# Layer two's adaLN chunks in two parts, six weight places before the first gather, and other latent norm chains

## The chip, the core and the metric

The kernel runs on one core of one Trainium2 chip. The metric is the time of one execution on the device in microseconds (us). Five engines work beside each other: TensorE (PE; its weight loads are listed as PEld), VectorE (DVE), ScalarE (ACT), GpSimd (POOL) and SyncE (SP), which here only issues transfers. The 16 DMA engines move the data.

## The reference

Two networks of two layers each, one behind the other, on 256 tokens of 1,024 float32 numbers. The first has a hybrid mixer and a PEER layer, in which each token picks 128 of 16,384 rows of two tables:

```python
def first_block(x, c, ...):
    c_act = jax.nn.silu(c)
    for l in range(DEPTH):                      # 2
        mod = c_act @ ada_w[l] + ada_b[l]       # 1024 x 6144
        sh1, sc1, g1, sh2, sc2, g2 = jnp.split(mod, 6, axis=-1)
        h = _modulate(x, sh1, sc1)
        mix = _hybrid_mixer(h, ...)
        x = _layer_norm(DEEPNORM_ALPHA * x + (1.0 + g1) * mix, ln1_g[l], ln1_b[l])
        h = _modulate(x, sh2, sc2)
        ffn = _peer(h, peer_wq[l], peer_k1[l], peer_k2[l], peer_u[l], peer_v[l])
        x = _layer_norm(DEEPNORM_ALPHA * x + (1.0 + g2) * ffn, ln2_g[l], ln2_b[l])
```

The second works on its result (the latents) and on 256 context tokens, which leave it after its first layer:

```python
h = modulate(rmsnorm(x, norm_pre_mix[i]), sh1, sc1)
mix = concat([windowed_gqa_with_context(...), fourier_mix(...)]) @ w_out[i]
x_mid = x + g1 * rmsnorm(mix, norm_post_mix[i])
hf = modulate(rmsnorm(x_mid, norm_pre_ffn[i]), sh2, sc2)
x = x_mid + g2 * rmsnorm(swiglu(hf, w_gate[i], w_up[i], w_down[i]), norm_post_ffn[i])
# and the same for xc, with csh1, csc1, cg1, ..., in layer 0
```

## The kernel before

Each engine has its own program, written out in one order; semaphores tie them together. In the code `b0` and `b1` are the layers of the first network, `c0` and `c1` the context's passes through the second, `l0` and `l1` the latents'.

**Order.** The head is `block1(0)`: mixer and routing of b0 for both tiles of 128 tokens. Then come the gathers: for each of four (layer, tile) pairs, 128 rows per token of table u (`dots`, L1611 on) and 128 of table v (`sums`, L1625 on). GpSimd issues one gather of 128 rows, 0.5 MB, for each pick (L1019) into one of nine slots; six of them are the tile `RING`. DVE uses the slots in order and gives each back. Beside this, DVE takes one step of another block's generator after fixed rounds of four picks (`stage`, the dictionaries at the end of the vector program): first c0's mixer while (0, tile 0) sums, then b1 tile by tile (`tile1`), then the rest of c0. When the gathers are over, l0 and l1 run alone.

**Weights.** PE asks for each weight chunk with `weight()` (L350); a chunk is up to 2,048 numbers on 128 partitions, 1 MB. The chunks lie in `W`, which has `NW = 3` places: chunk n goes to place n % 3, and SP issues it when chunk n - 3 has been read. SP's queue is the list `stream` in the order in which PE's program met `weight()`, `load_rows()` and `load()`; an entry that waits holds up all behind it. `load_rows` (L374) brings two rows of 1,024 to all partitions of `ROWS`; they wait until the two before have been read (`rows_read`).

**adaLN.** `ada(p, aw, whos, groups, beside)` (L419) multiplies the condition with 512 columns of the modulation weights at a time: a group is two chunks. FIRST and SECOND are four groups each (shift and scale of the first and second half of the layer), GATE1 and GATE2 two each. ACT copies each group's row to `ROWT`, PE turns it into columns (L437) or spreads it over the partitions (L443), and ACT copies that. With `beside`, a group also waits for a pick (`pace`, L414).

**Places that the change touches.** The keys of the routing (`SKN`) are loaded by an entry of `stream` behind b0's SECOND, with a wait for `(filled, len(order))`, that is for all banks opened so far (L577 to L579). b1's FIRST and SECOND run together, 16 chunks, before c0's mixer (L944); ACT takes seven of their copies, then `gelu(0, 0)`, then the rest (L1391 on). The latent norms are `stats`, `normalise` and `residual` (L1437, L1460, L2177): `bn_stats` of the rows, `bn_aggr`, the square of the mean, a root on ACT, a reciprocal, products with the gate row, an addition over both tiles, and then the same for the next norm. Between l0's two halves PE also has GATE1 of l1, and before l1 GATE2.

## Time and profile before

| | us |
|---|---|
| median of three runs (2920.5 to 2934.6) | 2928.4 |
| the profiled execution | 2932.3 |
| its span in the trace | 2930.5 |
| head, to the first gather | 267 |
| gathers and what runs beside them, to layer one's latents | 267 to 2,160 |
| latent blocks | 2,160 to 2,930 |

Busy over the span: PE 65%, DVE 62%, POOL 36%, ACT 13%. No engine is busy throughout, so the stretches have to be read one by one. In a timeline a row is one instruction or several alike in sequence; the number in brackets is the idle time of the engine before the first of them and what ended it. A DMA share of 1.03 or 1.04 is what the trace shows when all 16 engines are at work. The granted clock has two levels, 1.2 and 2.4 GHz, shown as 0.5 and 1.0.

### The profile page before, as it was taken

The page shows a single profiled execution, that of the slowest core. Times are in us where ns is not written, and L with a number is a line of the kernel's source. Part 1 is how long each engine was busy: PE and PEld are TensorE (multiplying, and loading weights), DVE is VectorE, ACT ScalarE, POOL GpSimd, SP SyncE. Part 2 cuts the span into 40 slices and gives each one's busy share as a digit, 9 for nine tenths or more (in the row PEclk, how much of TensorE's full clock was granted, in tenths as well). Part 3 has the DMA queues.
Part 4 walks back from the last instruction along what each step waited for, and adds up shares of the span by engine and source line. Part 5 has one row for each costly group of instructions (what it writes and reads, how often), then busy time and mean ns, then how long its engine had stood idle before and what let it go on. Part 6 is the DMA issues. An engine that isn't in the chain of part 4 may idle for free.

```text
span 2930.5 us, 23625 instructions
## 1 busy us (share of the span) xinstructions
PE 1910.9 (65%) x8197; PEld 1343.1 (46%) x8197; DVE 1819.2 (62%) x3305; ACT 367.6 (13%) x818; POOL 1064.6 (36%) x1045
## 2 busy tenths in 40 slices
PE   7889444356553363544444457868178999997998
PEld 4668111144442151132242145743157786476873
DVE  1434999678778878988879986676854200243001
ACT  1311101013102011012111010000013100030000
POOL 1002444457555555755566755455610000000000
PEclk9989655567766675867778877989579999998999
DMA  7367999989999999999999999999861544512443
GB/s 245 99 207 236 399 399 400 400 315 386 335 344 405 400 401 401 362 335 397 401 401 397 341 330 392 374 403 406 328 235 37 189 149 153 187 60 86 156 146 115
DMA packets 361766, 860.86 MB, mean 294 GB/s; under 512 B 23720, under 2 KB 148912, under 8 KB 361520
## 3 DMA queue, kind: packets, MB, share of 16 engines
q0 software_dynamic: 148000, 537.07, 47.8%
q1 hardware_dynamic: 213648, 322.29, 31.6%
q8 instruction: 65, 1.06, 0.1%
q14 instruction: 53, 0.43, 0.0%
HBM read 858.23 MB, written 1.05 MB: 293 GB/s over the span
## 4 chain that ended last, share of the span: by engine, by line
PE 36%; DMA 34%; DVE 15%; issue 10%; POOL 3%; ACT 2%; SPq 0%; DVEq 0%; ACTq 0%
PE bank L912 13%; DMA RING<-in_peer_v,EX 8%; PE bank L397 7%; DMA W<-in_ada_w 5%; DMA W<-in_w_ada 5%; PE bank L926 5%; DMA RING<-in_peer_u,EX 5%; DMA WORK<-in_peer_v,EX 3%; PE bank L406 3%; DMA W<-in_w_up 2%; POOL RING L1019 2%; DVE ACC L1639 2%; PE bank L429 2%; DMA W<-in_w_gate 2%; DVE hrows L1639 1%
## 5 line engine op out<-in xcount | busy, mean ns | idle before, releaser
L1019 POOL DMA_INDIRECT RING<-in_peer_u,EX x343 | 326.4, 952 | 569.6 <-DVE EX L1596 255.6
L912 PE MATMUL bank<-HT,W 128*128 128x256 f32 x2112 | 490.8, 397 | 54.1 <-DMA W<-in_w_up 28.9
L912 PEld LDWEIGHTS bank<-HT,W 128*128 128x128 f32 x2112 | 421.6, 200 | 123.1 <-DMA W<-in_w_up 32.2
L1019 POOL DMA_INDIRECT RING<-in_peer_v,EX x341 | 379.2, 1112 | 239.0 <-DVE hrows L1639 119.5
L1621 DVE SCALAR_TENSOR_TENSOR ACC<-RING,hrows 128x1024 bf16<-128x1024 f32 x343 | 406.2, 1218 | 79.4 <-DMA RING<-in_peer_u,EX 77.9
L429 PE MATMUL bank<-W,CACT 128*32 128x512 f32 x768 | 166.3, 969 | 271.0 <-DMA W<-in_w_ada 130.7
L397 PE MATMUL bank<-W,HT 128*128 128x256 f32 (+1 forms) x1120 | 250.1, 386 | 20.5 <-ACT HT L1071 7.4
L385 PE MATMUL bank<-consts,XN 128*128 128x128 f32 x208 | 44.6, 398 | 309.8 <-DVE XN L1710 149.5
L397 PEld LDWEIGHTS bank<-W,HT 128*128 128x128 f32 x1120 | 215.9, 195 | 53.9 <-issue 11.3
L926 PE MATMUL bank<-W,WORK 128*128 128x512 f32 x528 | 229.3, 597 | 14.3 <-DVE WORK L2209 14.3
L2209 DVE TENSOR_TENSOR WORK<-WORK,bank 128x256 f32<-128x256 f32 x66 | 27.2, 420 | 321.6 <-ACT WORK L1366 321.6
L1019 POOL DMA_INDIRECT WORK<-in_peer_v,EX x171 | 188.3, 1101 | 102.9 <-DVE hrows L1639 40.1
L1621 DVE SCALAR_TENSOR_TENSOR ACC<-WORK,hrows 128x1024 bf16<-128x1024 f32 x169 | 201.2, 1218 | 38.3 <-DMA WORK<-in_peer_u,EX 37.8
L1639 DVE SCALAR_TENSOR_TENSOR hrows<-RING,ACTS,hrows 128x1024 f32<-128x1024 f32 x154 | 198.2, 1287 | 37.1 <-DMA RING<-in_peer_v,EX 35.9
L1639 DVE SCALAR_TENSOR_TENSOR ACC<-RING,ACTS,ACC 128x1024 f32<-128x1024 f32 x155 | 198.6, 1281 | 32.6 <-DMA RING<-in_peer_v,EX 32.2
L1019 POOL DMA_INDIRECT WORK<-in_peer_u,EX x169 | 161.2, 954 | 156.9 <-DVE ACC L1621 132.3
L429 PEld LDWEIGHTS bank<-W,CACT 128*32 128x32 f32 x768 | 20.9, 135 | 364.3 <-DMA W<-in_w_ada 117.7
L385 PEld LDWEIGHTS bank<-consts,XN 128*128 128x128 f32 x208 | 38.8, 212 | 316.2 <-DVE XN L1710 151.7
L926 PEld LDWEIGHTS bank<-W,WORK 128*128 128x128 f32 x528 | 100.9, 192 | 141.3 <-issue 125.9
L621 PE MATMUL bank<-HT,W 128*128 128x128 f32 x832 | 118.4, 311 | 52.0 <-DMA W<-in_peer_wq 29.9
L621 PEld LDWEIGHTS bank<-HT,W 128*128 128x128 f32 x832 | 115.9, 226 | 56.1 <-DMA W<-in_peer_wq 26.6
L1054 ACT ACTIVATE WORK<-bank 128x512 f32<-128x512 f32 (+5 forms) x161 | 85.7, 546 | 434.2 <-PE bank L397 135.7
(343 smaller groups left out, 2289.2 us busy)
## 6 DMA issues: line engine op xcount, KB each, us to landing
W<-in_ada_w SPq DMA_DIRECT2D x48, 1024.0 KB, 13.5
W<-in_w_ada SPq DMA_DIRECT2D x48, 1024.0 KB, 16.5
W<-in_w_in SPq DMA_DIRECT2D x35, 1024.0 KB, 10.8
W<-in_w_gate SPq DMA_DIRECT2D x33, 1024.0 KB, 5.4
W<-in_w_up SPq DMA_DIRECT2D x33, 1024.0 KB, 5.6
W<-in_w_down SPq DMA_DIRECT2D x33, 1024.0 KB, 5.0
W<-in_peer_wq SPq DMA_DIRECT2D x24, 1024.0 KB, 16.5
W<-in_w_o SPq DMA_DIRECT2D x12, 1024.0 KB, 11.8
```

The source lines that it names most:

```text
L385: mm = pe.transpose(b[0:rows, j * P:(j + 1) * P], a, ident)
L397: mm = pe.matmul(b[:, t * 256:t * 256 + cols], hT[:, k, t * P:(t + 1) * P], w[:, k, 0:cols], start=(k == 0), stop=(k == K - 1))
L406: mm = pe.matmul(b[:, j * S:(j + 1) * S], w[:, k, j * P:(j + 1) * P], hT[:, k, :], start=(k == 0), stop=(k == DC - 1))
L429: mm = pe.matmul(b[32 * k:32 * k + 32, :], CACT[:, 4 * c + k, :], w[:, k, :], start=(c == 0), stop=(c == 1), skip_group_check=True)
L621: mm = pe.matmul(b[:, at:at + P], w[:, k, at:at + P], HT[:, 4 * c + k, T], start=first, stop=(c == 1 and k == 3), skip_group_check=True)
L912: mm = pe.matmul(bs[j][:, g * S:(g + 1) * S], w[:, k, j * P:(j + 1) * P], HT[:, k, :], start=(k == 0 and g == 0), stop=(k == DC - 1 and g ...
L926: mm = pe.matmul(bs[2 * t + hf][:, :], GU[:, 2 * c + k, t * P:(t + 1) * P], w[:, k, hf * 512:(hf + 1) * 512], start=(c == 0 and k == 0), s ...
L1019: gp.indirect_dma_start(SLOT[g % NS], None, rows, bass.IndirectOffsetOnAxis(EX[:, t, k:k + 1], 0))\
L1054: free(name, A(out_, b[:, :] if src is None else src(b), ACT.Copy, scale=scale))
L1621: ve.scalar_tensor_tensor(out=JUNK[:, g % 2, :], in0=SLOT[g % NS], scalar=1.0, in1=HB[:, :], op0=ALU.mult, op1=ALU.mult, accum_out=ACTS[:, ...
L1639: ins = ve.scalar_tensor_tensor(out=acc, in0=SLOT[g % NS], scalar=ACTS[:, k:k + 1], in1=acc, op0=ALU.mult, op1=ALU.add)
L2209: free(("gu", p, f), ve.tensor_tensor(GU[:, f, :], SG[:, f % 2, :], b[:, S:2 * S], ALU.mult))
```

## The change

1. **Six places.** For the first 36 chunks there are six places: the three of `W` and three more, each of two slots of `RING`. Chunk n waits for chunk n - 6. From chunk 36 on it is three again. The first six gathers wait for chunks 33 to 35. X, the late constants and ctx keep their places in SP's queue but for X (behind chunk 6, not 3) and the constants (behind 12, not 9).
2. **Keys.** b0's keys are issued by GpSimd when the last bank of b0's mixer is filled.
3. **b1's adaLN.** FIRST runs where FIRST and SECOND ran, with other paces; SECOND runs behind c0's mixer and ahead of tile one. `ln2` rows, asked for after it, move behind it in SP's queue.
4. **Latent norms.** The gate row is multiplied while the banks are read, one product per tile adds to X (`gated_residual`), and the next norm's squares are summed on ACT, tile by tile (`root_of_squares`). The output's store waits for both tiles.

```diff
@@ -102,6 +103,7 @@
+        WIDE = 36
@@ -252,7 +254,7 @@
-        w_landed = [sem(f"w_landed{i}") for i in range(NW)]
+        w_landed = [sem(f"w_landed{i}") for i in range(2 * NW)]
@@ -286,6 +288,20 @@
+        def place(n):
...
+            return n % (2 * NW) if n < WIDE else n % NW
...
+        def landed(n):
...
+            if n < WIDE:
+                return w_landed[place(n)], 16 * (n // (2 * NW) + 1)
+            return w_landed[place(n)], 16 * (WIDE // (2 * NW) + (n - WIDE) // NW + 1)
...
+        def held_before(n):
...
+            return n - 2 * NW if n < WIDE + NW else n - NW
@@ -351,11 +367,13 @@
-                view = W[:, n % NW, 0:k * cols].rearrange("p (k c) -> p k c", k=k)
+                at = place(n)
+                room = W[:, at, :] if at < NW else RING[:, 2 * (at - NW):2 * (at - NW) + 2, :].rearrange("p s n -> p (s n)")
+                view = room[:, 0:k * cols].rearrange("p (k c) -> p k c", k=k)
...
-                pe.wait_ge(w_landed[n % NW], 16 * (n // NW + 1))
+                pe.wait_ge(*landed(n))
@@ -574,9 +592,6 @@
-                load([(SKN[:, :, 0, :], d["peer_k1"][l].rearrange("h n d -> n h d")),
-                      (SKN[:, :, 1, :], d["peer_k2"][l].rearrange("h n d -> n h d"))],
-                     mark("skn", p), (filled, len(order)))
@@ -941,10 +956,11 @@
-            ada("b1", d["ada_w"][1], [0], FIRST + SECOND, beside=lambda i: gather(0, 0, 0, 5 * i + 80))
+            ada("b1", d["ada_w"][1], [0], FIRST, beside=lambda i: gather(0, 0, 0, 10 * i + 64))
...
+            ada("b1", d["ada_w"][1], [0], SECOND)
@@ -970,23 +986,23 @@
-                if e is chunks[NW]:
+                if e is chunks[2 * NW]:
...
-                if e is chunks[9]:
+                if e is chunks[12]:
...
-                    if n >= NW:
-                        sp.wait_ge(*chunks[n - NW]["free"])
-                    sp.dma_start(e["dst"], e["src"]).then_inc(w_landed[n % NW], 16)
+                    if held_before(n) >= 0:
+                        sp.wait_ge(*chunks[held_before(n)]["free"])
+                    sp.dma_start(e["dst"], e["src"]).then_inc(landed(n)[0], 16)
...
-            sp.wait_ge(mark("xu", "l1"), 2)
+            sp.wait_ge(mark("xu", "l1"), 2 * NT)
@@ -1006,6 +1022,10 @@
+            gp.wait_ge(filled, banks["mx", "b0", 3][0] + 1)
+            for e, keys in enumerate((d["peer_k1"], d["peer_k2"])):
+                gp.dma_start(SKN[:, :, e, :], keys[0].rearrange("h n d -> n h d")).then_inc(mark("skn", "b0"), 16)
@@ -1016,6 +1036,8 @@
+                            if g < NR:
+                                gp.wait_ge(*[e for e in stream if "dst" in e][WIDE - NW + g // 2]["free"])
@@ -1056,6 +1078,14 @@
+            def root_of_squares(p, i):
...
+                for t in range(NT):
+                    act.wait_ge(mark("xu", p), NT * (i - 1) + t + 1)
+                    do(A(XN[:, t, :], X[:, t, :], ACT.Square, accum_out=VE[:, t, 1:2]))
+                settle()
+                do(A(SD[:, :, 0], VE[:, :, 1], ACT.Sqrt, bias=const("eps"), scale=1.0 / D), mark("std", p if i == 1 else "l1"))
@@ -1282,7 +1312,10 @@
-                root(p, 1)
+                if p == "l1":
+                    root_of_squares("l0", 2)
+                else:
+                    root(p, 1)
@@ -1350,12 +1383,14 @@
-                root(p, 2)
+                root(p, 2 if p != "l1" else 1)
...
-                root(p, 3)
+                    root(p, 3)
+                else:
+                    root_of_squares(p, 1)
@@ -1388,12 +1423,10 @@
-            second = ada("b1", [0], FIRST + SECOND)
-            for _ in range(7):
-                next(second)
+            all_of(ada("b1", [0], FIRST))
...
-            all_of(second)
...
+            all_of(ada("b1", [0], SECOND))
@@ -1434,6 +1467,17 @@
+            def mean_squares(p, parts):
...
+                settle()
+                for t in range(NT):
+                    do(ve.bn_aggr(MV[:, t, :], parts[:, t, :, :]))
+                settle()
+                do(ve.tensor_tensor(VE[:, :, 0], MV[:, :, 0], MV[:, :, 0], ALU.mult))
+                settle()
+                do(ve.scalar_tensor_tensor(out=VE[:, :, 0], in0=VE[:, :, 0], scalar=RMS_EPS, in1=MV[:, :, 1],
+                                           op0=ALU.add, op1=ALU.add), mark("var", p))
@@ -2046,6 +2087,20 @@
+            def inverse_root(p, i):
...
+                ve.wait_ge(mark("std", p), i)
+                do(ve.reciprocal(RSD[:, :, 0], SD[:, :, 0]))
+                settle()
...
+            def rows_over_root(p, i):
...
+                inverse_root(p, i)
+                for t in range(NT):
+                    ins = ve.tensor_scalar(XN[:, t, :], X[:, t, :], RSD[:, t, 0:1], None, ALU.mult)
+                    do(ins, mark("y", p)) if t else do(ins)
+                settle()
@@ -2062,7 +2117,10 @@
-                normalise(p, 1, xs, RMS_EPS, True, XN, mark("y", p))
+                if p == "l1":
+                    rows_over_root("l1", 1)
+                else:
+                    normalise(p, 1, xs, RMS_EPS, True, XN, mark("y", p))
@@ -2172,30 +2230,42 @@
-                        free(("mx", p, j), ve.tensor_copy(XN[:, :, j * 256:(j + 1) * 256], two(b[:, :])))
+                        free(("mx", p, j), ve.tensor_tensor(XN[:, :, j * 256:(j + 1) * 256], two(b[:, :]),
+                                                            over_tiles(GA[:, gs[0], j * 256:(j + 1) * 256], 256), ALU.mult))
...
-                def residual(i, g, parts=None, names=None):
...
-                    if not names:
-                        settle()
-                    stats(p, i, XN, RMS_EPS, True, parts)
+                def residual(i, g):
...
+                    settle()
+                    stats(p, i, XN, RMS_EPS, True)
...
-                        for hf in range(2) if names else (0,):
-                            c = slice(hf * 512, (hf + 1) * 512) if names else slice(0, D)
-                            src = BK[banks[names[2 * t + hf]][0] % RB][:, :] if names else XN[:, t, :]
-                            ins = ve.scalar_tensor_tensor(out=XN[:, t, c], in0=src, scalar=RSD[:, t, 0:1], in1=GA[:, g, c],
-                                                          op0=ALU.mult, op1=ALU.mult)
-                            free(names[2 * t + hf], ins) if names else do(ins)
+                        do(ve.scalar_tensor_tensor(out=XN[:, t, :], in0=XN[:, t, :], scalar=RSD[:, t, 0:1], in1=GA[:, g, :],
+                                                   op0=ALU.mult, op1=ALU.mult))
...
-                residual(2, gs[0], ST4 if who == "l" else None)
...
+                def gated_residual(i, parts, names=()):
...
+                    mean_squares(p, parts)
+                    for k, name in enumerate(names):
+                        c = slice((k % 2) * 512, (k % 2 + 1) * 512)
+                        free(name, ve.tensor_tensor(XN[:, k // 2, c], wait_full(ve, name)[:, :], GA[:, gs[1], c], ALU.mult))
+                    settle()
+                    inverse_root(p, i)
+                    for t in range(NT):
+                        do(ve.scalar_tensor_tensor(out=X[:, t, :], in0=XN[:, t, :], scalar=RSD[:, t, 0:1], in1=X[:, t, :],
+                                                   op0=ALU.mult, op1=ALU.add), mark("xu", p))
...
+                    residual(2, gs[0])
...
-                normalise(p, 3, xs, RMS_EPS, True, XN, mark("y", p))
+                    normalise(p, 3, xs, RMS_EPS, True, XN, mark("y", p))
+                else:
+                    gated_residual(2, ST4)
+                    rows_over_root(p, 3)
```

SP's queue around b0's SECOND chunks and keys, before:

```order
L978 DMA XC<-in_ctx 128x2x1024
L983 DMA W<-in_w_o 128x8x256 x2
L988 DMA ROWS<-in_ln_g 128x1024
L988 DMA ROWS<-in_ln_b 128x1024
L983 DMA W<-in_ada_w 128x4x512 x8
L988 DMA WORK<-in_peer_k 128x8x128 x2
L983 DMA W<-in_peer_wq 128x8x256 x8
L983 DMA W<-in_ada_w 128x4x512 x4
```

and after:

```order
L999 DMA RING<-in_w_o 128x8x256 x2
L994 DMA XC<-in_ctx 128x2x1024
L999 DMA W<-in_w_o 128x8x256 x2
L1004 DMA ROWS<-in_ln_g 128x1024
L1004 DMA ROWS<-in_ln_b 128x1024
L999 DMA W<-in_ada_w 128x4x512
L999 DMA RING<-in_ada_w 128x4x512 x3
L999 DMA W<-in_ada_w 128x4x512 x3
L999 DMA RING<-in_ada_w 128x4x512
L999 DMA RING<-in_peer_wq 128x8x256 x2
L999 DMA W<-in_peer_wq 128x8x256 x6
```

The keys are gone from it, and between mixer and routing the chunks alternate between both kinds of places.

ACT from the copies of c0's mixer to the root of layer one's norm (128x1); ROWT and CR are adaLN copies, the roots are `SD<-VE`. Before:

```order
L1054 ACTIVATE XN<-bank 128x2x256 x4
L1058 ACT_TABLE_LOAD
L1058 ACTIVATE SD<-VE 128x2
L1063 ACTIVATE SD<-VE 128x1
L1269 ACT_TABLE_LOAD
```

After:

```order
L1076 ACTIVATE XN<-bank 128x2x256 x4
L1080 ACT_TABLE_LOAD
L1080 ACTIVATE SD<-VE 128x2
L1076 ACTIVATE ROWT<-bank 128x512 x2
L1076 ACTIVATE CR<-bank 128x4
L1076 ACTIVATE ROWT<-bank 128x512
L1076 ACTIVATE CR<-bank 128x4
L1076 ACTIVATE ROWT<-bank 128x512
L1076 ACTIVATE CR<-bank 128x4 x2
L1093 ACTIVATE SD<-VE 128x1
```

The eight adaLN copies of b1's SECOND now stand between c0's root (128x2) and layer one's root (128x1), which DVE's tile one begins with.

DVE in the middle of l1, from the last copy of the mixer's bank to the rows of the next norm. Before:

```order
L2175 COPY XN<-bank 128x2x256
L1447 BN_AGGR MV<-ST 128x2 x2
L1450 TENSOR_TENSOR VE<-MV 128x2
L1452 SCALAR_TENSOR_TENSOR VE<-VE,MV 128x2
L1457 RECIPROCAL RSD<-SD 128x2
L2188 SCALAR_TENSOR_TENSOR XN<-XN,RSD,GA 128x1024 x2
L2192 TENSOR_TENSOR X<-X,XN 128x2048
L1444 BN_STATS ST<-X 128x6 x4
L1447 BN_AGGR MV<-ST 128x2 x2
L1450 TENSOR_TENSOR VE<-MV 128x2
L1452 SCALAR_TENSOR_TENSOR VE<-VE,MV 128x2
L1457 RECIPROCAL RSD<-SD 128x2
L1464 TENSOR_SCALAR XN<-X,RSD 128x1024 x2
```

After:

```order
L2233 TENSOR_TENSOR XN<-bank,GA 128x2x256
L1474 BN_AGGR MV<-ST 128x2 x2
L1476 TENSOR_TENSOR VE<-MV 128x2
L1478 SCALAR_TENSOR_TENSOR VE<-VE,MV 128x2
L2093 RECIPROCAL RSD<-SD 128x2
L2258 SCALAR_TENSOR_TENSOR X<-XN,RSD,X 128x1024 x2
L2093 RECIPROCAL RSD<-SD 128x2
L2100 TENSOR_SCALAR XN<-X,RSD 128x1024 x2
```

The addition over both tiles and the second statistics are gone; ACT has two Squares in their place.

## Rows read from the trace of the kernel before

**Rows 1.** The page's slices: 40 equal parts of 73.3 us, busy tenths, DMA rate.

```profile
DVE  1434999678778878988879986676854200243001
...
DMA  7367999989999999999999999999861544512443
GB/s 245 99 207 236 399 399 400 400 315 386 335 344 405 400 401 401 362 335 397 401 401 397 341 330 392 374 403 406 328 235 37 189 149 153 187 60 86 156 146 115
```

**Rows 2.** Timeline of PE, head: start us, us, instruction, count, [idle before <-releaser].

```profile
32.04 1.52 PE L429 MATMUL bank<-W,CACT 128*32 128x512 f32 x8 [1.19 <-DMA W<-in_ada_w]
...
148.44 1.87 PE L429 MATMUL bank<-W,CACT 128*32 128x512 f32 x8 [3.69 <-DMA W<-in_ada_w]
...
152.91 2.78 PE L385 MATMUL bank<-consts,WORK 128*128 128x128 f32 x24
...
197.59 1.92 PE L429 MATMUL bank<-W,CACT 128*32 128x512 f32 x16
...
221.55 3.65 PE L385 MATMUL bank<-consts,XN 128*128 128x128 f32 x16
228.05 3.68 PE L385 MATMUL bank<-consts,WORK 128*128 128x128 f32 x16 [2.85 <-DMA WORK<-in_peer_k]
```

**Rows 3.** Timelines of ACT and of DVE, head.

```profile
147.04 0.57 ACT L1054 ACTIVATE ROWT<-bank 128x512 f32<-128x512 f32 x1
...
212.70 1.53 DVE L1466 TENSOR_SCALAR XN<-X,MV,RSD 128x1024 f32<-128x1024 f32 x2
```

**Rows 4.** Timeline of PE, layer two's adaLN chunks beside the gathers.

```profile
484.42 1.93 PE L429 MATMUL bank<-W,CACT 128*32 128x512 f32 x8 [5.64 <-DMA W<-in_ada_w]
...
536.70 1.93 PE L429 MATMUL bank<-W,CACT 128*32 128x512 f32 x8 [5.30 <-DMA W<-in_ada_w]
...
596.80 1.93 PE L429 MATMUL bank<-W,CACT 128*32 128x512 f32 x8 [5.53 <-DMA W<-in_ada_w]
```

**Rows 5.** Timeline of DVE, norm rows, residual, layer one's root.

```profile
580.95 1.28 DVE L1639 SCALAR_TENSOR_TENSOR ACC<-WORK,ACTS,ACC 128x1024 f32<-128x1024 f32 x1 [0.76 <-DMA WORK<-in_peer_v,EX]
600.80 4.63 DVE L2034 TENSOR_TENSOR GA<-GA,ROWS 128x1024 f32<-128x1024 f32 x4 [18.57 <-DMA ROWS<-in_norm_post_ffn]
...
785.86 2.47 DVE L1444 BATCH_NORM_STATS2 ST<-XN 128x6 f32<-128x512 f32 x4 [11.63 <-ACT XN L1054]
...
810.50 0.16 DVE L1693 RECIPROCAL RSD<-SD 128x1 f32<-128x1 f32 x1
```

**Rows 6.** Windows: us, busy of PE, PEld, DVE, ACT, POOL, clock, DMA share, GB/s.

```profile
786.00:805.00 19.00, 0.00 (x0) 0.00 (x0) 18.31 (x24) 1.34 (x3) 4.54 (x4) 0.61 0.70 252
805.00:844.00 39.00, 14.18 (x57) 9.69 (x58) 38.37 (x73) 6.49 (x13) 24.07 (x25) 0.63 0.79 286
```

**Rows 7.** Timelines of PE and of SP's queue before layer two's first tile.

```profile
821.89 1.97 PE L385 MATMUL bank<-consts,XN 128*128 128x128 f32 x8 [36.89 <-DVE XN L1710]
...
768.30 17.10 SPq L983 DMA_DIRECT2D W<-in_w_in  x3
```

**Rows 8.** Timeline of PE, starts behind three latent norms.

```profile
2297.87 2.90 PE L443 MATMUL bank<-ROWT,consts 128*128 128x512 f32 x4
...
2547.01 1.97 PE L385 MATMUL bank<-consts,XN 128*128 128x128 f32 x16
...
2683.53 3.67 PE L385 MATMUL bank<-consts,XN 128*128 128x128 f32 x16 [12.70 <-DVE XN L1464]
```

**Rows 9.** Timeline of DVE, layer two's middle and last latent norm.

```profile
2676.09 2.29 DVE L2192 TENSOR_TENSOR X<-X,XN 128x2048 f32<-128x2048 f32 x1
2678.42 2.47 DVE L1444 BATCH_NORM_STATS2 ST<-X 128x6 f32<-128x512 f32 x4
...
2921.05 2.73 DVE L2188 SCALAR_TENSOR_TENSOR XN<-bank,RSD,GA 128x512 f32<-128x512 f32 x4
2923.81 2.29 DVE L2192 TENSOR_TENSOR X<-X,XN 128x2048 f32<-128x2048 f32 x1
```

**Rows 10.** Timeline of ACT, an elementwise step over 1,536 columns.

```profile
112.01 1.48 ACT L1123 ACTIVATE WORK<-WORK 128x1536 f32<-128x1536 f32 x1
```

## What the change does to the time

> **What bounds the kernel now.** I read the page's slices first. They show three stretches [rows 1]: a head up to about 300 us, in which the DMA engines are mostly part idle; the gathers of the two PEER layers, up to about 2,130 us, in which the DMA row stands at 8 or 9 almost throughout and carries about 400 GB/s; and the latent blocks of the second network, to 2,930 us, where PE stands at 9 or 7. So each part of the change has to be costed in its own stretch. In the head the timeline of PE shows which waits end last. In the gathers a wait of DVE alone costs nothing if DMA works on through it, since the bytes are the same: there I ask how much DMA idle time goes away. In the latent blocks the gaps of PE between two blocks of matmuls count, and in each of them what ends last.
>
> **1. Six weight places and the keys, in the head.** Start: PE's last wait for a chunk of the first adaLN group ends at 32.04 us and is 1.19 us long [rows 2]. Until then DMA has had to bring the same eight chunks and X in either order, so more places bring nothing: 0, at most the 1.2 us of that wait, and as much in loss if X behind three more chunks mattered.
>
> GATE1: PE waits 3.69 us for a chunk until 148.44, works at the lower of its clocks, and begins the probabilities' transposes at 152.91 [rows 2]. The chunk had to wait for a place. With six it is there. What is late next is ACT, which is in exponentials and copies the first of the two rows at 147.04, done at 147.6 [rows 3]. The gate rows' broadcasts need that copy and took 2.8 us, so the transposes begin at about 150.3: 152.9 - 150.3 = 2.6 us; bounds 1.5 and 3.7 (the wait itself).
>
> SECOND: the transposes of the second modulated input start at 221.55, right behind the last SECOND group [rows 2]; their input XN was ready at 212.70 + 1.53 = 214.2 [rows 3]. With six places five of the eight chunks are there when PE arrives at 197.59 [rows 2], and the other three follow it at one transfer each, so the group ends near 212 and XN becomes the later one. That is 221.55 - 214.2 = 7.3 us. The ln1 rows stand ahead of the SECOND chunks in SP's queue and wait for the old rows to be read, which is over well before the mixer's last product, so the chunks are not blocked for long.
>
> Keys: PE then waits 2.85 us more for the keys until 228.05 [rows 2]. Before, their load stood in SP's queue behind a wait for the whole SECOND group; now GpSimd issues them when the mixer's last bank is filled (197.6), 16 us before XN. Its queue holds nothing else ahead of the first gather. That is 2.8 us; if the moved load were no earlier, 0. The places themselves cost nothing: they lie in the ring of gathers, whose first six uses now wait for chunks that are read before the first scores, so before any routing.
>
> Head: 2.6 + 7.3 + 2.8 = 12.7 us (10 to 17; the upper end if PE, less interrupted, also keeps its higher clock). From the first routing on DVE is busy and DMA full, both shifted alike, so the gain stays.
>
> The Trainium skill (page "DMA: Bandwidth & Descriptors", section "Issuing engines are not separate DMA queues") says that starting DMAs on several engines only saves the sequencer's time for issuing. By that the move of the keys to another queue would be worth nothing and the sum 2.8 us less. The rows speak for the other reading: it is the wait ahead of the load, not the engines that move it, that goes.
>
> **2. Four chunk pairs behind the context's mixer.** Now: the b1 chunks start in DMA-bound time. FIRST's first chunk is used at 484.42, its last at 536.70, SECOND's last at 596.80: 7.5 us each beside gathers [rows 4]. The norm rows stand behind all 16 in SP's queue, so DVE waits 18.57 us for them, until 600.80; just before, its sums come every 2.04 us (0.76 of it waiting) [rows 5]. After: the rows come behind FIRST, by about 545. The wait goes, and the last five sums before it come at 1.3 us, the 0.5 MB of a gather at 400 GB/s, instead of 2.04: 18.6 + 3 = 21.6. In the wait all nine slots had filled, a start that is now missing; I take off 1.6. The mixer's steps are tied to rounds of DVE's sums, so all of it, to the residual at 785.86, comes 20 us earlier (17 to 23).
>
> What is paid back: the eight chunks, 8.4 MB or 21 us at 400 GB/s, now have to pass between the mixer and layer two's first tile. In that place DMA has room: its share is 0.70 for 19 us and 0.79 for 39 us where a full one reads 1.03, so 19 x (1 - 0.70/1.03) + 39 x (1 - 0.79/1.03) = 6.1 + 9.1 = 15.2 us of idle [rows 6], and PE stands 36.9 us before tile one's transposes at 821.89 [rows 7]. I let the chunks use 12 of the 15; 21 - 12 = 9 us remain (6 to 21). On ACT the new copies stand ahead of the root that DVE uses at 810.50 [rows 5]. Chunks take the places from 768.30 on as the mixer's are read, three by 785.4 [rows 7]; with no gathers in the way until DVE is past the residual, the other five come at 3 to 4 us, the last by about 804, and the last column copy is at about 810. So DVE waits 0 to 4 us, which lies within the 9. Sum of part 2: -20 + 9 = -11 us (-17 to +4). It is the DMA idle time that shrinks by that much; DVE's 18.6 us would be the wrong number to take.
>
> **3. Latent norm chains.** Removed from each middle chain: an addition of 2.29 us and statistics of 2.47 us with about 0.9 us of small steps [rows 9]. Added: Square on ACT for two tiles, of which only the second lies behind DVE's last product. ACT needs 1.48 us for 1,536 columns [rows 10], so about 1.0 for 1,024, with 0.3 for the accumulator and the start. That is 5.6 - 1.3 = 4.3 us where the chain ends last. It does so in one place of four:
> - layer two's middle: PE stands 12.70 us before 2683.53 and waits for XN alone [rows 8]. 4.2 us.
> - layer one's middle: PE's own GATE1 group ends at 2297.87 + 2.90 = 2300.77 [rows 8], and the transposes start there. XN ready earlier changes nothing: 0.
> - between the layers: GATE2 holds PE until 2547.01 [rows 8], of which about 0.9 us was its last row copy standing behind the late root on ACT. The root now comes sooner: 0.9 us.
> - the end: before, products from 2921.05 (2.73 us) and the addition at 2923.81 (2.29 us), end 2926.10 [rows 9]. Now the four gate products run beside the root, from 2920.6 to 2923.3, then reciprocal and two products of 1.24 us: 2926.0. 0.
> Sum 5.1 us (3 to 7). The order of ACT shows no table load between Square and the root.
>
> **The sum.** -12.7 - 11 - 5.1 = -28.8 us. Against the profiled execution's 2932.3 us that gives 2903.5; this execution is 3.9 us above the median of 2928.4, so for the median **2899.6, say 2900 us**. The bounds of the terms taken together give -47 to -9. Nothing I found makes two of them fail together except the seam of part 2.
>
> **Rivals.**
> (a) More: the idle time at the seam is used up whole and PE keeps its clock in the head. -17 - 14 - 6 = -37, 2891 us. For it: the 15.2 us are measured. Against: three places cannot keep DMA full. A variant in which the norm chains pay in all four gaps adds 12 us, about 2888; PE's own groups in the gaps speak against it.
> (b) Less: an earlier start of the gathers is not an earlier end, since weight chunks that went out beside routing are now missing there. The head's 12.7 are lost: -16, 2912 us. For it: DMA stands at 9 from the fifth slice on, that is from 293 us [rows 1]. Against: the chunks ahead of DVE's position are the same.
> (c) No change or slower, one mechanism: the seam runs at the shared rate. If the eight chunks move at the 7.5 us each of [rows 4], beginning at 785.9, they end at 845.9, with the last columns at 849. DVE then waits 38 us for the root of layer one's norm, the sum of part 2 is -20 + 38 = +18, and the whole comes to 0: 2928 us. This is the point from which it decides. Beyond it, the three prefetched chunks of tile one are gone too, up to 3 x 7.5 = 22 us more: 2950 us, slower. For it: the order on ACT and PE is strict, and PE and DVE both stand behind it. Against: a DVE that waits stops the gathers after nine slots, and then the chunks have DMA alone.
> The Trainium skill (page "DMA: Bandwidth & Descriptors", section "Queues, rings and completion order") states that each DMA engine takes turns between the queues that have work, packet by packet. By that rule the shared rate holds exactly as long as gathers are queued; [rows 4] agree with it, and for the seam it would make (c) only if the gathers do not dry up.
> (d) The change doesn't do what it says: the first gathers wait for places in the ring, or DVE's gelu stands behind all of FIRST. The first case needs a chunk still unread when the first picks are routed, and the reads are ahead of the scores in PE's order. The second would show only if dots ended before FIRST; it costs a few us and falls into (b).
>
> **How the numbers follow.** Forecast, 2892 to 2910: 50%. (a), 2882 to 2892: 18%. (b) and (d), 2910 to 2922: 17%. (c) as no change, 2922 to 2936: 9%; (c) as slower, above: 6%. The range 2884 to 2918 holds the forecast and the nearer parts of (a) and (b), about 78%. A measurement of this kernel can tell about 0.5%, 14.6 us, from no change: faster means below 2913.8. The forecast, (a) and half of (b) lie there: 0.78. Slower, above 2943: 0.05. Within: 0.17.
>
> **What would show it.** Head: no DMA wait of PE between 140 and 230 us but a short one in SECOND; the transposes behind it released by DVE's XN, not by PE's own group; first dot of DVE about 12.7 us earlier. Gathers: DVE's wait for the norm rows gone; FIRST ends, the rows land before the gate products; between mixer and tile one chunks of b1 at 3 to 4 us each and a DMA share near 0.9 instead of 0.70 and 0.79; DVE's wait for ACT's root under 5 us. If that wait is 10 us or more, part 2 is wrong and (c) is at work. Latent: PE's gap before the second gate/up stretch 8.5 us instead of 12.70, the gaps in which GATE groups lie unchanged within 1 us. The stretch from first dot to last sum should be shorter by 11 us; if it is unchanged, the DMA idle time moved elsewhere.

## The result and the profile after

| | before | after |
|---|---|---|
| median, us | 2928.4 | 2889.9 (2887.4 to 2893.2) |
| profiled execution, us | 2932.3 | 2893.2 |
| its span, us | 2930.5 | 2891.4 |

The ratio is 0.9873, with a 95% interval of 0.9856 to 0.9890: 37 us less (32 to 42). The forecast was 2900, with a range of 2884 to 2918. The side and the range held. The median lies 2 us outside the band given to the forecast (2892 to 2910) and in the one given to rival (a), whose number was 2891. One of the six executions of e12_light_first below ran in a slower state (3615.7 us, granted clock 0.55 instead of 0.79) and is left out of its median. The gain of the profiled executions is 39.1 us against 28.8 in the sum, so some terms were too small.

The page's slices after, 72.3 us each, to be laid beside [rows 1]:

```profile
DVE  1436999889678889979889986676944200142001
...
DMA  8366999999999999999999999999860544512443
GB/s 288 111 217 226 399 399 401 369 376 374 371 402 404 400 401 391 336 368 399 399 403 374 339 348 392 368 405 405 323 237 30 189 150 156 189 61 90 157 146 116
```

The DMA row is full from the fifth slice to the twenty-eighth, without the dip to 315 GB/s in the ninth slice of [rows 1]. The picture is otherwise the same, so the shift of single instructions tells more. Below, each shift is the start in the trace after less the start of the same instruction before.

| instruction | shift, us | stretch, measured | forecast |
|---|---|---|---|
| last columns of layer one's first adaLN half, PE (33.49 and 33.50) | 0 | 0 | 0 |
| 29th to 113th dot of (0, tile 0) | -12.8 | -12.8 | -12.7 |
| residual behind c0's mixer, DVE | -38.3 | -25.5 | -20 |
| 169th to 225th sum, all in the next tile | -31.4 | +6.9 | +9 |
| last sum | -29.3 | +2.1 | 0 |
| first transposes of l0 | -31.8 | -2.5 | 0 |
| end | -39.1 | -7.3 | -5.1 |

**Head.** Timeline of PE after:

```profile
147.56 3.42 PE L461 MATMUL bank<-ROWT,consts 128*128 128x512 f32 x4 [2.06 <-ACT ROWT L1076]
150.77 3.08 PE L403 MATMUL bank<-consts,WORK 128*128 128x128 f32 x24
...
194.36 1.06 PE L447 MATMUL bank<-W,CACT 128*32 128x512 f32 x8
...
206.17 1.94 PE L447 MATMUL bank<-W,CACT 128*32 128x512 f32 x8 [3.83 <-DMA W<-in_ada_w]
208.80 1.94 PE L447 MATMUL bank<-RING,CACT 128*32 128x512 f32 x8 [0.70 <-DMA RING<-in_ada_w]
210.67 3.58 PE L455 MATMUL bank<-consts,ROWT 128*128 128x1 f32 x16
214.10 3.65 PE L403 MATMUL bank<-consts,XN 128*128 128x128 f32 x16
217.55 2.94 PE L403 MATMUL bank<-consts,WORK 128*128 128x128 f32 x16
```

GATE1 has no chunk wait; in its place stands the wait for ACT's row that the forecast named, and the transposes begin 2.1 us earlier (152.91 in [rows 2]). SECOND ends 7.5 us earlier than in [rows 2], and the keys' transposes follow with no wait, 10.5 us earlier (228.05 before). The transposes at 214.10 carry no bracket: they are released by PE's own group, not by XN.

**Gathers.** Timeline of DVE after, then of PE:

```profile
561.05 4.67 DVE L2075 TENSOR_TENSOR GA<-GA,ROWS 128x1024 f32<-128x1024 f32 x4
...
747.57 2.47 DVE L1488 BATCH_NORM_STATS2 ST<-XN 128x6 f32<-128x512 f32 x4 [14.45 <-ACT XN L1076]
778.05 0.16 DVE L1734 RECIPROCAL RSD<-SD 128x1 f32<-128x1 f32 x1 [5.76 <-ACT SD L1093]
```

```profile
772.28 1.93 PE L447 MATMUL bank<-W,CACT 128*32 128x512 f32 x8 [6.77 <-DMA W<-in_ada_w]
774.14 3.57 PE L455 MATMUL bank<-consts,ROWT 128*128 128x1 f32 x16
789.44 1.97 PE L403 MATMUL bank<-consts,XN 128*128 128x128 f32 x8 [11.73 <-DVE XN L1751]
```

The gate products at 561.05 stand where 600.80 stood in [rows 5], and the 18.57 us are gone. In place of PE's 36.89 us of [rows 7], PE now works on the eight chunks and waits 11.73. DVE has a new wait of 5.76 us.

Windows after (columns as in [rows 6]): ahead of and behind the gate products, then from the mixer's end on:

```profile
536.00:550.00 14.00, 0.00 (x0) 0.00 (x0) 13.41 (x23) 0.37 (x1) 5.72 (x5) 0.50 0.77 268
...
577.00:600.00 23.00, 16.16 (x68) 14.13 (x69) 22.55 (x28) 4.56 (x10) 14.91 (x13) 0.75 0.96 349
...
747.00:778.00 31.00, 18.43 (x96) 7.62 (x88) 24.00 (x32) 4.99 (x12) 8.29 (x8) 0.64 1.03 385
778.00:811.00 33.00, 13.43 (x59) 9.55 (x60) 31.52 (x61) 6.52 (x14) 19.08 (x21) 0.66 0.95 352
```

The seam is full: 1.03 and 0.95 where [rows 6] have 0.70 and 0.79.

**Latent blocks.** Timeline of PE, then of ACT, after, in layer two's middle:

```profile
2646.28 3.67 PE L403 MATMUL bank<-consts,XN 128*128 128x128 f32 x16 [8.44 <-DVE XN L2100]
```

```profile
2641.90 1.06 ACT L1086 ACTIVATE XN<-X 128x1024 f32<-128x1024 f32 x1 [1.62 <-DVE X L2258]
2642.86 0.19 ACT L1086 ACTIVATION_READ_ACCUMULATOR XN<-X 128x1 f32 x1
2643.10 1.06 ACT L1086 ACTIVATE XN<-X 128x1024 f32<-128x1024 f32 x1
```

The gap is 8.44 us instead of the 12.70 of [rows 8], and Square takes 1.06 us with 0.19 us for reading its sum, against 1.0 + 0.3 in the forecast.

### The profile page after: what moved, and what is told of

It reads as the page before. It is cut to its first block, busy times and chain, and to the rows that moved or that the text cites. A ratio compares the mean times of both kernels' runs of the same rounds, so it can differ in the third digit from the quotient of the medians.

```text
span 2891.4 us, 23615 instructions
## 1 busy us (share of the span) xinstructions
PE 1891.9 (65%) x8197; PEld 1332.9 (46%) x8197; DVE 1803.3 (62%) x3281; ACT 374.6 (13%) x830; POOL 1071.4 (37%) x1047
## 3 DMA queue, kind: packets, MB, share of 16 engines
q1 hardware_dynamic: 211568, 321.24, 31.9%
q8 instruction: 65, 1.06, 0.2%
## 4 chain that ended last, share of the span: by engine, by line
PE 36%; DMA 33%; DVE 14%; issue 11%; POOL 3%; ACT 2%; SPq 0%; DVEq 0%; ACTq 0%
PE bank L927 13%; DMA RING<-in_peer_v,EX 10%; PE bank L415 8%; DMA W<-in_w_ada 6%; PE bank L941 5%; DMA W<-in_ada_w 4%; DMA RING<-in_peer_u,EX 3%; PE bank L424 3%; DMA WORK<-in_peer_u,EX 3%; DMA W<-in_w_up 2%; DVE ACC L1680 2%; POOL RING L1041 2%; PE bank L447 2%; DMA W<-in_w_gate 2%; DMA WORK<-in_peer_v,EX 2%
## 5 line engine op out<-in xcount | busy, mean ns | idle before, releaser
L927 PE MATMUL bank<-HT,W 128*128 128x256 f32 x2112 | 482.0, 392 | 61.6 <-DMA W<-in_w_up 30.3
L927 PEld LDWEIGHTS bank<-HT,W 128*128 128x128 f32 x2112 | 414.8, 197 | 128.6 <-DMA W<-in_w_up 33.9
L447 PE MATMUL bank<-W,CACT 128*32 128x512 f32 x704 | 149.9, 955 | 237.5 <-DMA W<-in_w_ada 135.3
L415 PE MATMUL bank<-W,HT 128*128 128x256 f32 x992 | 228.7, 394 | 18.6 <-ACT HT L1101 7.4
L415 PEld LDWEIGHTS bank<-W,HT 128*128 128x128 f32 x992 | 195.8, 198 | 50.6 <-issue 10.2
L636 PEld LDWEIGHTS bank<-HT,W 128*128 128x128 f32 x832 | 115.6, 225 | 55.9 <-DMA W<-in_peer_wq 26.6
```

The lines of the kernel that those rows point to most:

```text
L415: mm = pe.matmul(b[:, t * 256:t * 256 + cols], hT[:, k, t * P:(t + 1) * P], w[:, k, 0:cols], start=(k == 0), stop=(k == K - 1))
L447: mm = pe.matmul(b[32 * k:32 * k + 32, :], CACT[:, 4 * c + k, :], w[:, k, :], start=(c == 0), stop=(c == 1), skip_group_check=True)
L636: mm = pe.matmul(b[:, at:at + P], w[:, k, at:at + P], HT[:, 4 * c + k, T], start=first, stop=(c == 1 and k == 3), skip_group_check=True)
L927: mm = pe.matmul(bs[j][:, g * S:(g + 1) * S], w[:, k, j * P:(j + 1) * P], HT[:, k, :], start=(k == 0 and g == 0), stop=(k == DC - 1 and g ...
```

## The experiments

Twelve kernels ran in three groups of four (e5 and e11 are the changed kernel again); the kernels of a group ran on one chip, beside the kernel before. These chips spread more than the one above: before had 2925.6 to 2946.8 us in 17 executions beside the first group. So a ratio carries some 0.2 to 0.3%, and one trace may differ from the next by 10 us in the gathers. I take sizes from ratios, and from a trace only what holds over a long stretch or is a single wait.

| kernel | median, us | before beside it | ratio, 95% | us below before |
|---|---|---|---|---|
| e1_places_keys | 2927.7 | 2937.7 | 0.9958 (0.9942 to 0.9974) | 12.3 |
| e2_split | 2922.1 | 2937.7 | 0.9931 (0.9911 to 0.9951) | 20.3 |
| e3_norms | 2931.2 | 2937.7 | 0.9968 (0.9948 to 0.9989) | 9.4 |
| e4_keys_in_queue | 2909.5 | 2937.7 | 0.9899 (0.9882 to 0.9916) | 29.7 |
| e5_after_again | 2904.5 | 2939.6 | 0.9878 (0.9848 to 0.9908) | 35.9 |
| e6_light_chunks | 2892.3 | 2939.6 | 0.9849 (0.9822 to 0.9876) | 44.4 |
| e7_rows_only | 2923.1 | 2939.6 | 0.9940 (0.9920 to 0.9960) | 17.6 |
| e8_roots_store | 2899.0 | 2939.6 | 0.9861 (0.9835 to 0.9888) | 40.9 |
| e9_light_old_place | 2907.1 | 2928.8 | 0.9918 (0.9899 to 0.9936) | 24.0 |
| e10_rows_first | 2891.5 | 2928.8 | 0.9872 (0.9851 to 0.9893) | 37.5 |
| e11_after_third | 2897.2 | 2928.8 | 0.9891 (0.9873 to 0.9908) | 31.9 |
| e12_light_first | 2894.7 | 2928.8 | 0.9875 (0.9855 to 0.9895) | 36.6 |

The last column is one less the ratio, times before's median.

### One part at a time

e1 is the kernel before with `WIDE`, `place`, `landed`, `held_before`, the waits of the first gathers and the keys on GpSimd. e2 has only the two pieces that split b1's adaLN. e3 has only the latent norms. All three are pieces of the diff above, unchanged.

> The kernel before with the six weight places and the keys on GpSimd, nothing else. My theory: the head is 12.7 us shorter and the gathers keep it, so 2915.7 us against 2928.4 (11 to 15 less). Rival: the gathers are bound by their DMA bytes from a point that does not move, and the head is lost: 2926 to 2928. In the trace the first dot should come 12 to 13 us earlier and the last sum by the same amount; by the rival the last sum by 0 to 3 us.

> The kernel before with b1's SECOND behind the context's mixer, nothing else. The forecast's own sum was -20 + 9 = -11, so 2917 us. A ledger of DMA time, drawn from the trace of the changed kernel, gives more: ahead of the mixer's end 8.4 MB less (21 us) and 5 us less idle DMA, behind it 9 us paid back, so -17 and 2911 us. Rival (the seam at the shared rate): 2926 to 2930. It tells whether the surplus over the forecast lies in this part or in two parts helping each other.

> The kernel before with the latent norm chains of the change, nothing else. Forecast -5.1: 2923 us. The trace of the changed kernel has 7.3 us less from the latents' first transposes to the end, which would be 2921. Rival (the chain pays in all four gaps): -17, 2911 us.

e1 gives 12.3 us (8 to 17). That speaks for a head whose gain stays to the end and against rival (b), a head that is lost. Its trace does not show the sign that was named for it: against the trace before, the first dot is 12.2 us earlier, but the last sum only 0.1 us, which is the rival's sign; the 10 us go between the residual (9.7 us earlier) and the end of the next tile's dots (2.0), in DMA that stands idle more (37.2 us from the 29th dot to the 169th sum, where the trace before has 27.6). The trace is of the slowest of e1's six executions (2933.7 us), on a chip where the kernel before is 9 us slower than on the first one, and of that kernel no trace was taken there. So rival (b) is refused by the times and not by the trace. e2 gives 20.3 (14 to 26), above the -11 of the forecast and in reach of the ledger's -17. e3 gives 9.4 (3 to 15); that interval holds 5 and 7 and leaves out the rival's 17, and the traces below do better. The three sum to 42 us, the whole change has 37 (32 to 42): no sign that the parts need each other.

### The keys by SyncE's queue

```diff
-            gp.wait_ge(filled, banks["mx", "b0", 3][0] + 1)
-            for e, keys in enumerate((d["peer_k1"], d["peer_k2"])):
-                gp.dma_start(SKN[:, :, e, :], keys[0].rearrange("h n d -> n h d")).then_inc(mark("skn", "b0"), 16)
...
+                load([(SKN[:, :, 0, :], d["peer_k1"][l].rearrange("h n d -> n h d")),
+                      (SKN[:, :, 1, :], d["peer_k2"][l].rearrange("h n d -> n h d"))],
+                     mark("skn", p), (filled, len(order)))
```

> The changed kernel with b0's keys back in SyncE's queue behind the SECOND chunks; six places stay. Theory: the wait ahead of the load costs, whichever engine issues it: PE waits about 3 us for the keys again and all behind it is later, 2893 us against 2890. Rival (by the Trainium skill, DMA: Bandwidth & Descriptors, Issuing engines are not separate DMA queues, another issuing engine brings nothing but its time to issue): 0, 2890 us. The chunk order in the head is the same in both.

Timelines of PE and of SP's queue in e4:

```profile
214.93 3.35 PE L403 MATMUL bank<-consts,XN 128*128 128x128 f32 x16
221.23 3.62 PE L403 MATMUL bank<-consts,WORK 128*128 128x128 f32 x16 [2.95 <-DMA WORK<-in_peer_k]
...
215.10 0.99 SPq L1007 DMA_DIRECT2D WORK<-in_peer_k  x2
```

The wait is back with 2.95 us, beside 2.85 in [rows 2]. The load is issued at 215.10, when SECOND's last bank is filled; in the changed kernel GpSimd issues it at 194.73. The medians do not settle 3 us, this row does: what costs is the 20 us later issue. e4 gives back the old wait, the old queue and the old place in it at once, so it does not tell these apart; the issuing itself takes 0.99 us in the row above. The Trainium skill (page "DMA: Bandwidth & Descriptors", section "Issuing engines are not separate DMA queues") puts only the time for issuing on the engine. No row here speaks against that: the move to GpSimd paid because it took the load out from behind a wait, as the prediction had argued.

### The wait or the bytes

e7 is the changed kernel with SECOND ahead of the context's mixer, but behind the norm rows:

```diff
+            ada("b1", d["ada_w"][1], [0], SECOND)
             c0 = block2("c0", 0, "c")
             next(c0)
-            ada("b1", d["ada_w"][1], [0], SECOND)
```

and the two lines of ACT swapped alike.

> The changed kernel with b1's SECOND ahead of the context's mixer again, but behind the norm rows in SyncE's queue. DVE's wait for the rows stays away, the 8.4 MB come back to where they were. If the gain of part 2 was the row wait (the -20 of the forecast was read from it), this is as fast as the changed kernel, within 3 us. If the gain was idle DMA time at the seam, that idle (12 of 15.2 us) comes back: 8 to 12 us more than the changed kernel. If PE reaches the mixer so late that DVE's steps wait for it, still more, up to the whole 17 us of part 2.

It is 18.6 us above the changed kernel of its chip (2923.1 and 2904.5): all of part 2 is gone, though the rows come early (the gate products start at 560.78). In their traces the dots and sums of the next tile stand 17 us apart, once 2 us of the head are taken off. Timeline of DVE in e7, and a window behind its mixer:

```profile
607.19 0.17 DVE L1498 RECIPROCAL RSD<-SD 128x2 f32<-128x2 f32 x1 [25.34 <-ACT SD L1080]
...
778.00:811.00 33.00, 1.97 (x8) 1.57 (x8) 32.31 (x49) 6.19 (x13) 15.15 (x15) 0.50 0.61 198
```

Behind every wait stood the same chunks. Before, DVE waited 18.57 us for rows queued behind them; here it waits 25.34 for a root of ACT that stands behind their copies. And the DMA engines idle at the seam again: share 0.61. So this run does not separate the row wait from the place of the bytes, as it was meant to; it shows that taking away the named releaser alone brings nothing.

### The price of the chunks in either place

In e6 (the changed kernel) and e9 (the kernel before) only 64 of the 512 columns of each of the eight SECOND chunks are loaded. PE multiplies as before, with old numbers in the rest, so only the time counts. The edit of e6, which e9 has in the code of the kernel before:

```diff
+                    if light[0] <= n < light[1]:
+                        dst, src = dst[:, :, 0:64], src[:, :, 0:64]
```

> The changed kernel with 64 of 512 columns loaded for each of b1's eight SECOND chunks (7/8 of their bytes left out, the places hold old numbers otherwise): 7.3 MB less, 18 us of DMA at 400 GB/s. It measures what the chunks cost where they now stand. The forecast's seam (12 of 15.2 us of idle DMA filled, 9 us paid back): 7 to 9 us less than the changed kernel. Rival, no DMA idle is used up and the bytes are paid in full: 18 us less. Rival, hidden altogether: 0.

> The kernel before with 64 of 512 columns loaded for each of b1's eight SECOND chunks, which stand where they stood, ahead of the norm rows (7.3 MB left out, 18 us of DMA at 400 GB/s; the places hold old numbers otherwise). It prices the chunks in the old place, as e6 did in the new one. A ledger of DMA time: the bytes, 18 us, and the idle DMA that DVE's row wait made (10.1 us at 600 to 640), so 26 to 28 us less than before. If the row wait alone counted, as the forecast took it: 20 to 22. If only the bytes counted: 18.

Against e5, e6 is 8.5 us faster by the ratios, 12.2 by the medians and 9.3 by the means of five executions each (2 to 17), which leaves out both 18 and 0. Its trace has the next tile's dots 6 to 7 us earlier than e5's. So 18 us of bytes cost about 8 at the seam. In the old place they cost 24 us (19 to 30). That is below the 26 to 28 of the ledger, inside its interval, and does not tell it from the 20 to 22 of the row wait; 18 is just outside. The difference, about 16 us by the ratios for seven eighths of the bytes, is part 2 measured a third way: e7 against e5 is 35.9 - 17.6 = 18.3 us, and the trace after has 25.5 - 6.9 = 18.6.

e12 cuts the FIRST chunks of the changed kernel instead, with the same two lines.

> The changed kernel with 64 of 512 columns loaded for each of b1's eight FIRST chunks, which stand beside layer one's first dots (7.3 MB left out). By the ledger of DMA time a chunk beside gathers costs its bytes, 2.3 us for 7/8 of one, whatever PE or DVE wait for: 18 us less than the changed kernel, at once and to the end. Rival, chunks beside gathers are hidden behind DVE (its dots come at 1.2 us each when rows are there): under 9 us.

A miss. The ratio gives 4.7 us, the medians 2.5, and the rival (under 9 us) holds. In the trace the first sum comes 12 us earlier than in e11 (2.6 us of the head taken off); 56 sums later 4 us of it are left, and in the next tile nothing. Windows of e12 and a row of its DVE timeline:

```profile
460.00:519.00 59.00, 22.92 (x102) 9.27 (x100) 58.29 (x123) 8.07 (x15) 35.61 (x39) 0.59 0.92 334
519.00:545.00 26.00, 0.00 (x0) 0.00 (x0) 17.71 (x33) 1.59 (x2) 11.88 (x11) 0.50 0.76 285
...
778.00:811.00 33.00, 14.93 (x65) 10.82 (x65) 30.30 (x60) 6.94 (x16) 17.77 (x19) 0.66 0.76 277
...
780.19 0.16 DVE L1739 RECIPROCAL RSD<-SD 128x1 f32<-128x1 f32 x1 [17.97 <-ACT SD L1098]
```

DVE is busy 58.29 of 59 us and DMA stands at 0.92: without chunks DVE is the bound. Most of the freed time turns up as idle DMA: 6 us in the first window, 7 in the second, 9 at the seam, where DVE now waits 17.97 us (over the stretch from the 29th dot to the 169th sum 26.0 us of idle, where e11 has 10.6). Freed bytes are a gain only if something is ready to use them.

### Waits at the seam

e8 is the changed kernel with three edits: `root1("b0", 0, 5)` of ACT is taken after five of SECOND's eight steps, `root("l0", 1)` after six of the last adaLN's, and the store goes tile by tile. e10 has the `ln2` rows ahead of SECOND in addition.

```diff
-            all_of(ada("b1", [0], SECOND))
+            second = ada("b1", [0], SECOND)
+            for _ in range(5):
+                next(second)
+            root1("b0", 0, 5)
+            all_of(second)
...
-            ada("b1", d["ada_w"][1], [0], SECOND)
             load_rows(d["ln2_g"][0], d["ln2_b"][0])
+            ada("b1", d["ada_w"][1], [0], SECOND)
```

> The changed kernel once more, on the same chip as the three beside it, as their measure. Expected: 1.2 to 1.5% below before.

> The changed kernel with three waits taken out: ACT computes layer one's root ahead of the last SECOND copies (DVE waited 5.76 us for it), l0's first root ahead of its last two column copies (PE waited 2.00 us for XN), and the output is stored tile by tile. If DMA bounds the seam (its share there is 1.03 in the changed kernel), the first brings 0 and the whole 2 + 1.3 = 3 us. Rival, DVE bounds the seam: 5.8 more, 9 us.

> The changed kernel with the three edits of e8, and the ln2 rows loaded ahead of b1's SECOND chunks, so that DVE waits neither for ACT's root nor for rows between the mixer and tile one (5.8 us in the changed kernel, 10 in e8). If DMA bounds the seam, the sum is that of e8 plus 1 or 2 us of idle DMA: 3 to 5 us less than the changed kernel. Rival, DVE bounds it: 9 to 13 us less.

> The changed kernel once more, as the measure of the kernels beside it on this chip. Expected: 1.2 to 1.5% below before.

Timeline of DVE in e8, then in e10:

```profile
778.31 1.28 DVE L1750 SCALAR_TENSOR_TENSOR X<-X,MV,ROWS 128x1024 f32<-128x1024 f32 x1 [9.97 <-DMA ROWS<-in_ln_b]
```

```profile
773.75 0.16 DVE L1743 RECIPROCAL RSD<-SD 128x1 f32<-128x1 f32 x1 [2.57 <-ACT SD L1094]
...
788.92 0.16 DVE L1743 RECIPROCAL RSD<-SD 128x1 f32<-128x1 f32 x1 [4.75 <-ACT SD L1094]
```

Each wait taken away is followed by the next: for rows behind the chunks, then for the next root behind the copies of the last chunks. From the end of the mixer's bank (745.64) to tile one's transposes (789.99) e10 takes 44.4 us; e11 takes 42.0 (752.35 to 794.36). Two waits of DVE less did not shorten it, as the theory has it that bytes set the seam. The chunks show how: with DVE waiting less, the last four of e10 were used 7.0, 3.7 and 6.8 us apart (762.67, 769.68, 773.35, 780.11), where the changed kernel had most at 2.6 to 3.7. What e8 does gain is elsewhere: PE's wait ahead of l0's transposes is 0.39 us instead of 2.01 in e5, and from the start of DVE's last products to the end of the span it takes 5.7 us instead of 6.9. By the medians e8 and e10 are 5.4 and 5.8 us below the changed kernel of their chips, with intervals that hold 0. They cannot choose between 3 us and the 9 of e8's rival; e10's rival (9 to 13) is refused by the seam's length alone. It is the best version that I have, by some 3 us that the rows show.

## Why the prediction was right, and where it was not

**Head, -12.7 forecast, -12.8 measured in this pair of traces, about 9 over all.** The agreement is partly luck. GATE1: 2.6 forecast, 2.1 at the transposes; in this pair PE then stayed at the higher clock for more of the values' products (5.54 us from 154.74 instead of 8.44 from 156.58), and the mixer's end is 3.2 us earlier (194.36, before 197.59). SECOND: the step that failed is "XN becomes the later one". XN was ready at 211.0; of the last three chunks, issued from 194.5 on when the mixer's places came free, the last landed only at 208.8, beside the keys and the first routing weights. PE's wait for a chunk was 3.83 us there, not a short one, and its columns ended at 214.1. Of the 7.3 us, 4.2 came here. Keys: 2.8 forecast, 2.95 in e4's row. The rest up to -12.4 at the first dot came behind the keys, where PE works more at the higher clock (window 215 to 235: granted 0.88; the same work before, 225 to 245: 0.78). The prediction put the gain at up to 17 "if PE, less interrupted, also keeps its higher clock"; that cause made up for a step too large.

Over all traces, the head stands four times in its old form (before, e2, e3, e9) and nine times in its new one (all others but e4). The first dot starts at 265.6 to 272.2 us in the old ones, of which the trace before is the latest, and at 257.6 to 262.6 in the new ones. The means are 9.1 us apart: 0.5 at the mixer's end, 3.9 more in SECOND, 2.9 for the keys, 1.7 in the routing behind them. So the head gives about 9 us, just under the range of 10 to 17. GATE1's term came out near 0, SECOND's at half, and only the keys' was right.

**Part 2, -20 + 9 = -11 forecast, -25.5 + 6.9 measured, -18.6.** This is the term that was mis-sized. The mechanism, idle DMA time filled at the seam, was right. The step that failed is the -20. I read it from DVE's wait and five sums, against my own rule that only idle DMA counts. The same rule, applied after the result, gives it: 8.4 MB less ahead of the mixer's end, 21 us, and the idle DMA of that wait. That was a window of the trace before that I had not weighed:

```profile
600.00:640.00 40.00, 19.01 (x81) 16.79 (x82) 38.50 (x41) 6.18 (x13) 23.05 (x19) 0.63 0.77 260
```

40 x (1 - 0.77/1.03) = 10.1 us, of which 3.5 + 1.6 come back in the windows after. 21 + 10.1 - 5.1 = 26, measured 25.5. Over these windows together: idle before 10.1 + 15.2 = 25.3 us, after 3.5 + 1.6 + 2.6 = 7.7, so 17.6 us of idle less and 18.6 us of time. The whole stretch, from the 29th dot to the 169th sum, says the same: thirty equal windows over it give 27.6 us of idle DMA before and 9.2 after, 18.4 less.

Here the size does not hang on one pair of traces. Seven traces have SECOND behind the mixer with all its bytes (after, e2, e4, e5, e8, e10, e11), three have the old order (before, e1, e3). By the means of these, the stretch from the 29th dot to the residual is 26.0 us shorter, the one from there to the 169th sum 7.4 longer: 18.6 in all, with 16.8 us less of idle DMA (12.7 against 29.5). As a forecast this ledger of DMA time lies inside the intervals of e2 and e9, which are wide, and it missed e12, which shows its limit: it holds while DVE can keep up.

**The seam.** Forecast 12 of 15.2 us filled and 9 paid back; 6.9 measured, and 2.1 more by the last sum. The last chunk came 24.7 us behind the start of the residual's statistics (772.28 - 747.57), not 18, and DVE waited 5.76 us for ACT's root, not 0 to 4. The second to the fifth chunk were used 2.6 to 3.7 us apart, with DMA nearly to themselves; the last 7.8 us behind the one before it (764.44), when DVE was giving slots back to the gathers again. That agrees with the Trainium skill (page "DMA: Bandwidth & Descriptors", section "Queues, rings and completion order"), by which queues with work take turns. Rival (c), all eight at 7.5 us, did not happen, for the reason given against it: a DVE that waits lets the gathers dry up.

**Latent norms, -5.1 forecast, -7.3 measured in this pair, 6.4 over all.** Layer two's middle 4.3 (4.2 forecast), between the layers 0.9 (0.9), layer one's middle 0.2 (0), the end 0.4 (0). Only the first is a wait that all traces repeat (12.70 us with the old chains, 8.44 with the new ones); the others are smaller than what the same stretches differ by from trace to trace. The 1.5 us that I missed lie behind the middle gap, in the gate and up products: 152.18 us instead of 153.66. Windows of before, then of after, from the first of these products, 4 us each:

```profile
2688.50:2692.50 4.00, 3.98 (x12) 3.33 (x13) 1.25 (x2) 1.07 (x1) 0.00 (x0) 0.63 0.02 4
```

```profile
2651.30:2655.30 4.00, 4.00 (x19) 3.54 (x20) 1.22 (x1) 1.01 (x1) 0.00 (x0) 1.00 0.01 4
```

In this pair the same work is granted 0.63 behind a gap of 12.70 us and 1.00 behind one of 8.44. All four traces with the long gap are low (before 0.63, e1 0.50, e2 0.57, e9 0.59; products 153.66 to 155.24 us), and nine of ten with the short one are at 1.00 with 152.18 or 152.19 us. The tenth is e12, with the same gap of 8.44 us before 2655.02 and products of 153.62 us:

```profile
2660.00:2664.00 4.00, 3.99 (x12) 3.33 (x13) 1.24 (x2) 1.06 (x1) 0.00 (x0) 0.63 0.02 4
```

So the gap's length alone does not decide the level, and the 1.5 us come in most executions, not in all. The whole stretch from l0's transposes to the end is 767.6 to 770.5 us in the four traces with the old chains, and in the eight with the new ones and the old store 760.4 to 762.9 but for e12's 766.2: 6.4 us between the means. The term was a little too small, by the clock that the prediction did not count.

**The bounds and the rivals.** The lower ends of the three terms, 17, 17 and 7, make -41, not the -47 of the prediction; the measured -37 lies inside either. Rival (a) had the total right, -37, and its direction: more of the seam's idle time was used (all but 2.6 of 15.2 us) and PE kept its clock better in the head. But most of what part 2 gave above the forecast came ahead of the mixer's end, a gain that (a) does not name.

**Left open.** The last sum stands 2.1 us later against its neighbours than before, and the first latent transposes 2.5 us earlier: the two nearly cancel, and other traces of the same kernel move them both ways, so I give them no cause.

## What to carry over

In a stretch that the DMA engines bound, cost a move in DMA time from start to end: bytes taken from one side, bytes added to the other, idle share on both; here an engine's wait pointed to the place and not to the price. Before taking a named releaser away, ask what else stands behind the same transfer, since the next wait in line will take its place. And check the other bound: where the computing engine is already at its limit, as DVE in e12, removed bytes buy little. And do not trust a term because one pair of traces repeats it: the head's -12.8 was 9 over thirteen traces.

## What was not expected of the hardware

A pause of PE can cost more than its length: in the 9 us from the transposes on, the trace before has level 0.5 for all of the first 5 and three quarters of the next 4, the trace after for 3.6 us in all; that is worth the 1.5 us. It need not save it when it is shorter: e12, with the short pause, has the clock of the trace before. And where no chunk was in the way (e12, window 460 to 519), DVE's dots came every 1.14 us, ahead of the 1.3 us that 0.5 MB take at 400 GB/s: DMA had bound them with little to spare.
